# The clearing of a DRAM scratch room is issued from GpSimd's queue instead of ScalarE's

## The reference

```
def first_block(x, ...):
    h = rmsnorm(x, norm_mix_pre[l])
    (c_q, c_kv, k_r, sg_u, sg_v, cv_x, cv_b, cv_c, pool_in, gate_pre) = split_cols(h @ w_in[l])
...
def hierarchical_moe(...):           # the end of third_block
    slot_tok = jnp.full((cap,), n_tok, jnp.int32).at[dest].set(tok_sorted)
    ...
    x_pad = jnp.concatenate([xt, jnp.zeros((1, d), xt.dtype)], axis=0)
    xb = x_pad[slot_tok].reshape(n_blocks, MOE_BLOCK, d)
```

## Time and profile before

| what | value |
|---|---|
| median of 3 runs | 3441.1 us (3439.76 to 3442.41) |
| the profiled execution | 3439.76 us |
| its span, first to last instruction | 3438.1 us |
| TensorE busy | 3130.9 us, 91% |
| VectorE, ScalarE, GpSimd busy | 1248.4, 654.6, 126.0 us |
| granted TensorE clock, mean | 0.937 |
| DMA moved | 420.33 MB, of it 23.59 MB written to DRAM |

### The profile page before, as it was taken

One profiled execution on the slowest core, in us unless ns is written; L12 is line 12 of the kernel. 1 busy time (PEld: TensorE's weight loads), 2 busy tenths in 40 slices (PEclk: granted clock), 3 DMA queues, 4 the chain that ended last, 5 costly groups with the idle time before them and its releaser, 6 DMA issues. The chain is left out here.

```text
span 3438.1 us, 36291 instructions
## 1 busy us (share of the span) xinstructions
PE 3130.9 (91%) x14114; PEld 1999.4 (58%) x14114; DVE 1248.4 (36%) x2368; ACT 654.6 (19%) x1500; POOL 126.0 (4%) x148
## 2 busy tenths in 40 slices
PE   8789998999999889887999999998859996899997
PEld 4368756874478544683488844786645754333332
DVE  1554425310042754154243302324654133333334
ACT  1121113210010630470010000013531121111110
POOL 1000000000000200001000000000010011000000
PEclk9889999999999989897999999898869997999998
DMA  9111221222222001201222221122001304999995
GB/s 359 50 67 57 74 79 50 98 80 73 77 72 98 25 25 50 74 1 37 74 74 75 97 86 60 66 98 74 1 26 55 117 15 180 423 424 424 425 422 229
DMA packets 120924, 420.33 MB, mean 122 GB/s; under 512 B 6705, under 2 KB 35778, under 8 KB 99282
## 3 DMA queue, kind: packets, MB, share of 16 engines
q1 hardware_dynamic: 112882, 379.48, 28.8%
q10 hardware_dynamic: 3024, 23.59, 1.7%
q0 software_dynamic: 4880, 15.35, 1.3%
HBM read 394.81 MB, written 23.59 MB: 122 GB/s over the span
## 5 line engine op out<-in xcount | busy, mean ns | idle before, releaser
L750 PE MATMUL bank<-arena 128*128 128x256 f32 x4480 | 980.1, 382 | 6.1 <-PEq L131 3.2
L750 PEld LDWEIGHTS bank<-arena 128*128 128x128 f32 x4480 | 860.5, 192 | 128.4 <-issue 12.5
L423 PE MATMUL bank<-arena 128*128 128x512 f32 x1504 | 657.9, 600 | 10.3 <-PEq L932 5.3
L423 PEld LDWEIGHTS bank<-arena 128*128 128x128 f32 x1504 | 289.3, 193 | 372.3 <-issue 372.3
L176 PE MATMUL bank<-arena 128*128 128x512 f32 (+9 forms) x1384 | 461.5, 493 | 47.3 <-PEq L2744 11.6
L176 PEld LDWEIGHTS bank<-arena 128*128 128x128 f32 (+3 forms) x1384 | 247.9, 198 | 255.7 <-issue 231.5
L3184 DVE TENSOR_TENSOR arena<-arena,bank 128x512 f32<-128x512 f32 x128 | 87.8, 688 | 139.2 <-PE bank L3088 136.8
L497 DVE SCALAR_TENSOR_TENSOR arena<-arena,bank 128x512 f32<-128x512 f32 x32 | 20.6, 684 | 311.7 <-PE bank L423 311.7
L3088 PE MATMUL bank<-arena 128*128 128x512 f32 x256 | 122.9, 615 | 4.4 <-DVE arena L3170 4.4
L3060 PE MATMUL bank<-arena 128*32 128x512 f32 x1024 | 115.7, 595 | 11.1 <-DMA arena<-in_moe_w_up_dram 11.1
L201 DVE COPY arena<-bank 128x512 f32<-128x512 f32 (+11 forms) x64 | 30.9, 490 | 236.8 <-PE bank L176 201.7
(11 more groups left out here) (478 smaller groups left out, 3214.1 us busy)
## 6 DMA issues: line engine op xcount, KB each, us to landing
arena<-in_moe_w_gate_dram SPq DMA_DIRECT2D x64, 1024.0 KB, 16.6
arena<-in_moe_w_up_dram SPq DMA_DIRECT2D x64, 1024.0 KB, 18.8
arena<-in_moe_w_down_dram SPq DMA_DIRECT2D x32, 2048.0 KB, 24.1
arena<-in_w_in_dram SPq DMA_DIRECT2D x29, 2048.0 KB, 7.9
arena<-in_w_ff_dram SPq DMA_DIRECT2D x16, 2048.0 KB, 8.7
x_slots<-arena ACTq DMA_DIRECT2D x8, 2048.0 KB, 32.8
arena<-in_w_out_dram SPq DMA_DIRECT2D x8, 2048.0 KB, 7.9
arena<-in_w_gate_dram SPq DMA_DIRECT2D x11, 1024.0 KB, 5.4
```

Source lines behind the costliest of these rows:

```text
L423: last = pe.matmul(c.banks[2 * i + half][:, :], hidden[:, k0 + k, i * P:(i + 1) * P], w[:, k, half * 512:(half + 1) * 512], start=k0 + k = ...
L750: last = pe.matmul(bank[:, m, :], lhsT, rhs, start=fresh and m == 0 and k == 0, stop=k == 3, skip_group_check=True)
```

## The change

`clear_slots` moves from ScalarE's stream to GpSimd's, still in the first block and still after `columns_ready`. GpSimd makes the zeros there, waits for them and for the columns, and issues the same nine DMAs. ScalarE keeps only its part of the norms. The memset of the zeros comes after the wait for the other constants instead of before it.

```diff
@@ setup_constants
-    zeros, zeroed = c.region(9, 0, UNIT), c.sig("zeros_made")
...
             pool.memset(c.ones[:, :], 1.0).then_inc(set_.sem, set_.up())
-            pool.memset(zeros, 0.0).then_inc(zeroed.sem, zeroed.up())
             pool.wait_ge(set_.sem, set_.at(3))
+            clear_slots(c, pool, columns_ready)
...
-            act.wait_ge(columns_ready.sem, columns_ready.at(2))
-            act.wait_ge(zeroed.sem, zeroed.at(1))
-            clear_slots(c, act, zeros)
...
-def clear_slots(c, act, zeros):
-
-    cleared = c.sig("slots_cleared")
+def clear_slots(c, pool, parameters):
+
+    zeros = c.region(9, 0, UNIT)
+    made, cleared = c.sig("zeros_made"), c.sig("slots_cleared")
     c.x_slots = c.nc.dram_tensor("x_slots", ((MAX_PAIRS + 1) * PAIR, D), F32).ap()
     room = c.x_slots.rearrange("(p r) n -> p (r n)", p=P)
+    pool.memset(zeros, 0.0).then_inc(made.sem, made.up())
+    pool.wait_ge(made.sem, made.at(1))
+    pool.wait_ge(parameters.sem, parameters.at(2))
     for at in range(0, room.shape[1], UNIT):
         n = min(UNIT, room.shape[1] - at)
-        act.dma_start(room[:, at:at + n], zeros[:, 0:n]).then_inc(cleared.sem, cleared.up(16))
+        pool.dma_start(room[:, at:at + n], zeros[:, 0:n]).then_inc(cleared.sem, cleared.up(16))
```

## The result

The changed kernel takes 3488.76 us (median of 4 runs, 3486.46 to 3490.83), the kernel before 3441.56 (4 runs, 3439.76 to 3442.41). The ratio is 1.0138, 95% interval 1.012 to 1.0155: slower by 47.2 us, where I had forecast 3440.8 within 3437.5 to 3445.7. The forecast is wrong.

The account below looks back on a forecast made before the run. TensorE, busy 91%, bounds the kernel; the edit acts only on the opening, set by ScalarE's ninth issue. -0.25 us on 3439.76 gives 3439.5; the runs' median lies 1.34 above that execution, so 3440.8, range 3437.5 to 3445.7.

Parts of the forecast that it names:

- the sum for GpSimd's issues: Opening block: nine issues of 0.57 us, 5.13 in all, from 15.95 to 21.08; TensorE starts at 21.54.
- the exit of 0.46: End of the opening block: TensorE starts 0.46 us after the last issue ends, read as 21.79 - 21.33.
- Hogging: Rival: clears on GpSimd's queue nearly stop the loads, so `pool` lands at 63.6; +13 to +15, 3455; chance 0.04.
- the full queue: Rival: GpSimd's queue has no room for 4 KB pieces, TensorE starts near 43.5; +22, 3462.8; chance 0.04.
- The cost of the issues: Opening block, GpSimd: 0.57 us for each clearing issue of 128 rows, 5.13 us for nine.
- the far bounds of 0.88 and 0.99: Dearer GpSimd issues: 0.88 us each gives +2.5; 0.99, the indirect issues, another operation, gives +3.5.
- The lock-out: Rival: VectorE's eight products keep GpSimd from issuing until 20.83, TensorE starts at 26.42; +4.6 us, 3445.7; chance 0.04.
- the row at 3052.92: A GpSimd issue overlapping a VectorE copy by 0.09 us still takes 0.53; cited for adding nothing for VectorE.
- Who gets turns: Clearing and load queues alternate packets one for one; clears flow 4 to 5 us after issue, `pool` near 34; cost nothing.
- The memset: GpSimd's 4096-wide memset, 3.50 us, moved later but ending near 6, before the columns are ready; cost nothing.
- The select: GpSimd's select at L1114, behind the small loads, starts between 62 and 75, up to 17 us late; cost nothing.
- The gain: Opening block: TensorE starts at 21.54 instead of 21.79, 0.25 us earlier; at most 0.50, set by VectorE's floor.

Follow-up runs that it names:

- e3: The changed kernel with GpSimd issuing only the first of the nine clears and ScalarE the other eight; 3451.13 us, ratio 1.0028 to the kernel before.
- e5: The changed kernel with GpSimd issuing the first four of the nine clears and ScalarE the other five; 3482.52 us, ratio 1.0122 to the kernel before.
- e1: The changed kernel with its opening block opened with no_gpsimd_drain=True, clears still on GpSimd; 3438.45 us, ratio 0.9992 to the kernel before.
- e4: The changed kernel with zeros and clears moved into the next block, `tables`, behind GpSimd's thirteen small loads; 3441.61 us, ratio 1.0002 to the kernel before.

## Why the prediction was wrong

**The step that failed** is in the sum for GpSimd's issues: "from 15.95 to 21.08; with the exit of 0.46 TensorE starts at 21.54". The 0.46 us were read behind ScalarE's last *issue*: its clears were still under way for 50 us at that exit, and nothing waited. I carried this over to GpSimd as if an exit were an exit. Behind GpSimd's issues it comes 0.4 to 0.7 us after the last *landing* (after, e3, e5), and e1 shows that it is the form of the exit that makes it so. The term of 0.46 us should have been 46.7 + 0.7 - 0.53, about 46.9 us after the last issue's end.

Could the trace of before have told it? It has no exit at which a GpSimd transfer is under way: in `tables` GpSimd waits itself for its loads and for the clears (L1117) before it leaves, and in the kernel's text every other stream of GpSimd that issues transfers waits for them in its own block too. So the row was missing, as the row for the issue's cost was. But for the issue I gave bounds from both sides, and for the exit none. My own sentence on the kernel before, that nobody waits for the landing in this block, was the assumption to be priced: the clears' landing, up to 71.5 us before, was in the trace, so the bound of this case was to be had, 71.5 - 21.3 = some 50 us.

**The rivals** all put the loss in the wrong place. Hogging (3455) and the full queue (3462.8) end on the right side, still well short of 3488.76, but neither happened: e1 keeps all of the traffic and loses nothing. That several rivals for "slower" had small chances each, and all of one kind (traffic), hid that the kind "waits for landing" had no chance at all.

**The cost of the issues** was right: 4.90 us for nine, 0.54 each, where I took 0.57; the far bounds of 0.88 and 0.99 didn't come.

**The lock-out** didn't come. VectorE's eight products fill 15.10 to 19.97, GpSimd's issues start at 15.73 and take 0.532 to 0.677 us, 4.90 in all. In e4, where VectorE makes one copy of 0.69 us beside them, the nine take 0.532 to 0.577, 4.76 in all. In the row at 3052.92 this rested on an overlap of 0.09 us; now it rests on 4.2 us. The rule of the Trainium skill ("SBUF — State Buffer", the "DVE blocks DMA" trap) is stated for VectorE in a two-port mode, and the same page of the Trainium skill, under "Who interferes with whom", says that `tensor_tensor`, the operation of these products, has no such mode. So the prediction applied the rule to products that it does not cover. The trace agrees with the page as it stands, and no run here tests the trap itself.

**Who gets turns** was right. Queues of the changed kernel, 22 to 60 us, packets, MB, share:

```profile
q0 software_dynamic: 998, 14.52, 89.2%
q1 hardware_dynamic: 1000, 1.72, 11.7%
```

One for one, with 16 KB rows against rows of 2 KB or less, as ScalarE's queue had it. GpSimd's queue neither hogs nor runs full. It has no packet from 16 to 18 us and the first near 19.7, so the clears begin to flow some 4 us after the first issue, at the near end of the 4 to 5 that I took. `pool` lands 23.7 and `latents` 56.9 us after their issue (24.7 and 62.0 in the earlier trace rows); in e1, where it matters, the products run on without a gap.

**The memset** cost nothing, and ScalarE, free sooner, gained nothing: both as argued. **The select** was forecast for 62 to 75; in e1 it starts at 76.93, a little later, and is hidden.

**The gain** was sized 0.25 us. Where the exit doesn't wait (e1, e4), TensorE starts 0.9 to 1.0 us earlier than 21.79. In e1, 0.42 us of that are only that VectorE was done at 20.41 (15.54 + 4.87) in that execution instead of 20.83; and TensorE follows VectorE's end by 0.40, without waiting for GpSimd's last issue. The gain stays too small to be told in the total.

## What to carry to other kernels

Before a DMA issue moves to another engine, ask at each block exit behind it whether that engine's transfers are still under way there, and what it costs if the exit waits for their landing: an issue is not a landing. Where the trace has no row for that engine at such an exit, price both cases; here the costly one was the time to landing, known from the same transfers on the old queue. A large transfer that nobody needs soon can stay on GpSimd if it is issued at the start of a long block, as e4 does, or if the exit is of the form in e1.

## What the hardware showed that I had not expected

A block's exit in its ordinary form treats the issuers differently. ScalarE's clears, under way for 50 us, held nothing; of GpSimd's, one held the exit to 32.94, four to 62.57 and nine to 67.50, each 0.4 to 0.7 us after the last landing. With the other form of the exit (e1) they hold nothing either.

After 51.66 us of idling TensorE restarts no worse than after 5.10. The window from 67 has a granted clock of 0.74, but it opens 0.5 us ahead of the first product; cut at the first product, eight microseconds have 0.77 (67.5 to 75.5), and in the kernel before 0.78 (21.8 to 29.8). During the idle it shows 0.50, the lower of the two levels, 1.2 GHz.

Three queues share as two do, packet for packet (105, 106, 105 in e5). This made the cost steep at the start: one clear of nine on GpSimd costs 11.15 us of late start, four already 40.78.
